# Row sums of squares moved into the last output tile, one modulation sum moved, and idle products reshaped, in a three-block transformer kernel

## The reference

```
for i in range(2):                       # first_block
    mod = silu(c) @ ada_w[i] + ada_b[i]  # sh1, sc1, g1, sh2, sc2, g2
    h = rmsnorm(x, norm1_g[i]) * (1 + sc1) + sh1
    y = attention_i(h)                   # i=0: window + sinks, i=1: stick breaking
    x = x + g1 * y
    h = rmsnorm(x, norm2_g[i]) * (1 + sc2) + sh2
    x = x + g2 * ((silu(h @ w_gate[i]) * (h @ w_up[i])) @ w_down[i])
u = rmsnorm(x, norm_mix_w)               # second_block
x = x + hybrid_mixer(u)
x = x + conv_gated_mlp(rmsnorm(x, norm_ffn_w))
return rmsnorm(x, final_norm_w)
```

## Time and profile before

| | |
|---|---|
| median of three runs | 2357.7 us |
| the profiled execution, its own time | 2357.86 us |
| its span, first to last instruction | 2356.0 us |
| PE busy / weight loads busy | 2289.3 us (97%) / 1830.7 us (78%) |
| DVE / ACT / POOL busy | 1170.3 / 870.5 / 163.1 us |
| mean granted clock of TensorE | 0.992 |

### The profile page before, as it was taken

The page is one execution under the profiler, slowest core; times in us unless marked ns, Lnnn a source line. Parts: engine busy times, 40 slices in busy tenths (PEclk is TensorE's granted clock), DMA queues, the critical chain, the costliest instruction groups (busy, mean ns, idle before and its releaser), DMA issues.

```text
span 2356.0 us, 27370 instructions
## 1 busy us (share of the span) xinstructions
PE 2289.3 (97%) x11168; PEld 1830.7 (78%) x11168; DVE 1170.3 (50%) x1621; ACT 870.5 (37%) x1413; POOL 163.1 (7%) x145
## 2 busy tenths in 40 slices
PE   7988999999999999999999999999999999999998
PEld 4767788888777677888887877866778887888886
DVE  5764655543465744333335455556744345553453
ACT  3653322222354533322323236356363223332331
POOL 2111000000100010000010002022020001000001
PEclk9999999999999999999999999999999999999999
DMA  9422465633212122232232222211223222233222
GB/s 339 141 90 84 167 223 196 212 110 99 81 63 72 48 70 88 91 99 99 91 106 81 98 91 95 98 59 63 72 90 108 98 81 99 90 98 107 93 87 81
DMA packets 77517, 250.67 MB, mean 106 GB/s; under 512 B 8272, under 2 KB 16720, under 8 KB 77392
## 3 DMA queue, kind: packets, MB, share of 16 engines
q1 hardware_dynamic: 77392, 248.93, 31.4%
HBM read 244.70 MB, written 4.19 MB: 106 GB/s over the span
## 4 chain that ended last, share of the span: by engine, by line
PE 88%; ACT 5%; DVE 4%; issue 1%; POOL 1%; DMA 0%; POOLq 0%; DVEq 0%; SPq 0%; ACTq 0%
PE pb L755 26%; PE pb L759 26%; PE pb L757 25%; PE pb L967 1%; PE pb L992 1%; PE pb L800 1%; PE pb L977 1%; PE pb L943 1%; ACT slab L1371 1%; ACT whi L1118 1%; PE pb L779 1%; PE pb L775 1%; PE pb L777 1%; ACT spare L1371 1%; PE pb L1042 1%
## 5 line engine op out<-in xcount | busy, mean ns | idle before, releaser
L755 PE MATMUL pb<-hhi,whi 128*128 128x512 f32 x1976 | 785.7, 398 | 5.0 <-ACT hhi L1146 3.0
L1410 DVE TENSOR_TENSOR wlo<-raw,whi 128x1024 fp32r<-128x1024 f32 x361 | 446.4, 1241 | 673.2 <-ACT whi L1118 673.1
L757 PE MATMUL pb<-hhi,wlo 128*128 128x512 f32 x1976 | 770.5, 390 | 1.7 <-DVE wlo L1410 1.7
L759 PE MATMUL pb<-hlo,whi 128*128 128x512 f32 x1976 | 771.0, 390 | 0.4 <-DVE hlo L1406 0.4
L1118 ACT ACTIVATE whi<-raw 128x1024 fp32r<-128x1024 f32 x361 | 379.2, 1056 | 728.7 <-PE pb L759 712.0
L755 PEld LDWEIGHTS pb<-hhi,whi 128*128 128x128 f32 x1976 | 370.8, 188 | 98.1 <-issue 24.3
L759 PEld LDWEIGHTS pb<-hlo,whi 128*128 128x128 f32 x1976 | 370.7, 188 | 81.4 <-DVE hlo L1406 1.6
L757 PEld LDWEIGHTS pb<-hhi,wlo 128*128 128x128 f32 x1976 | 371.1, 188 | 78.9 <-DVE wlo L1410 2.7
L755 PE MATMUL pb<-ahi,whi 128*128 128x512 f32 x848 | 336.6, 397 | 1.4 <-ACT ahi L1300 0.7
L759 PE MATMUL pb<-alo,whi 128*128 128x512 f32 x848 | 331.9, 391 | 0.0
L757 PE MATMUL pb<-ahi,wlo 128*128 128x512 f32 x848 | 331.5, 391 | 0.0
(11 more groups left out here) (231 smaller groups left out, 1686.0 us busy)
## 6 DMA issues: line engine op xcount, KB each, us to landing
raw<-stream SPq DMA_DIRECT2D x361, 512.0 KB, 3.3
slab<-ada_w SPq DMA_DIRECT2D x80, 512.0 KB, 4.9
early<-ada_w SPq DMA_DIRECT2D x32, 256.0 KB, 8.5
X<-xT SPq DMA_DIRECT2D x8, 256.0 KB, 4.8
ya<-slab SPq DMA_DIRECT2D x8, 256.0 KB, 2.7
slab<-ya SPq DMA_DIRECT2D x8, 256.0 KB, 4.7
outT<-X SPq DMA_DIRECT2D x8, 256.0 KB, 2.1
cst<-consts SPq DMA_DIRECT2D x1, 576.0 KB, 8.6
```

Of the source, the lines that this page charges most:

```text
L755: e.matmul(out, wh, hi, start=s.k == 0, stop=False)
L757: e.matmul(out, wl, hi, start=False, stop=False)
L759: i = e.matmul(out, wh, lo, start=False, stop=s.last)
L1410: e.tensor_tensor(wlo[:, u % NW, :], raw[:, u % NRAW, :], whi[:, u % NW, :].bitcast(F), ALU.subtract).then_inc(*v_cut.up(u))
```

## The change

`gemm` takes the number of the norm that follows as `hold`, and emits a new tick `sums` behind block k = K - 3 of its last output tile. `sums` holds the first half of the old `total`; `total` keeps the second half. For norm 0 and the group norms `sums` stands directly ahead of `total`, as before. `modsum(11)` moves to the end of the `mods()` generator, two generator steps behind the last `fma`; the generator is woven into the feed-forward product, one step to six blocks. `warm` issues two matmuls, with 512 and 256 columns, in place of one with 512.

```
@@ gemm
             self.tick("mm", Step(u, b, k, k == K - 1, tile, src(k), rows))
+            if hold and (k, m) == (K - 3, len(outs) - 1):
+                self.tick("sums", hold)
@@ mods
                 tick("fma", 8 * j + k)
                 yield 1
+        yield 1
+        tick("modsum", 11)
@@ rstd, norm (and the same for norm 6)
     def rstd(sid):
+        if sid == 0 or isinstance(sid, tuple):
+            tick("sums", sid)
         tick("total", sid)
...
-        tick("warm", 1)
+        tick("warm", 768)
         rstd(n)
-        tick("warm", 1)
+        tick("warm", 768)
         tick("spread", n)
-        tick("warm", 1)
+        tick("warm", 768)
@@ project, project_first, ffn
-        run(gemm(src, K, outs(4), "m", then=squares, hold=True))
+        run(gemm(src, K, outs(4), "m", then=squares, hold=n))
...
-                                    hold=part and d0 == 4)
+                                    hold=n + 1 if part and d0 == 4 else None)
@@ ahead of norm(2)
     run(mod)
-    tick("modsum", 11)
@@ tensor
-        def total(sid):
-            b = take(("stat", sid))
+        def sums(sid):
+            b, n = take(("stat", sid)), nstat(sid)
             w.wait_ge(d_in, "vec")
-            n = 3 if isinstance(sid, tuple) else 7
             w.wait_ge(v_norm if sid == 0 else p_sum, (sid, n - 1))
             for c in range(4):
-                i = e.matmul(b[:, c:c + 1], acc[:, quarter(c)], C("one"), start=c == 0, stop=False, skip_group_check=True)
+                e.matmul(b[:, c:c + 1], acc[:, quarter(c)], C("one"), start=c == 0, stop=False, skip_group_check=True)
+
+        def total(sid):
+            b, n = bank(("stat", sid)), nstat(sid)
             w.wait_ge(a_sq, (sid, n))
             for c in range(4):
                 i = e.matmul(b[:, c:c + 1], sq_of(sid, n)[:, quarter(c)], C("one"), start=False, stop=True, skip_group_check=True)
...
             b = take("warm")
-            for _ in range(n):
-                e.matmul(b, ident, cst[:, 0:S], start=True, stop=True)
+            for m in (S, n - S):
+                e.matmul(b[:, 0:m], ident, cst[:, 0:m], start=True, stop=True)
```

More of the change, by code:

```diff
@@ L121, in release, with gemm @@
         self.held.clear()
-    def gemm(self, src, K, outs, order="k", rows=P, evac=None, then=None, hold=False):
+    def gemm(self, src, K, outs, order="k", rows=P, evac=None, then=None, hold=None):
         M = range(len(outs))
@@ L328, in project_first @@
         order += [(k, m) for m in range(5, 8) for k in range(KD)]
-        steps = gemm(lambda k: ("oa", k), KD, [("wo_a", P * i, ("res", 0, i)) for i in range(8)], order, then=squares, hold=True)
+        steps = gemm(lambda k: ("oa", k), KD, [("wo_a", P * i, ("res", 0, i)) for i in range(8)], order, then=squares, hold=1)
         def as_ready():
@@ L1070, in output @@
             give(("y", g, j), v_ssd, ("y", g, j))
-        do = {"mm": mm, "mr": mr, "evac": evac, "modsum": modsum, "pre": pre, "premod": premod, "total": total, "warm": warm, "spread": spread, "norm": norm,
+        do = {"mm": mm, "mr": mr, "evac": evac, "modsum": modsum, "pre": pre, "premod": premod, "sums": sums, "total": total, "warm": warm, "spread": spread, "norm": norm,
               "tables": tables, "kstat": lambda: head_stats("k"),
```

## The result

The changed kernel took 2362.84 us in the median of 16 runs (2359.35 to 2364.97), the kernel before 2357.8 us beside it (2355.22 to 2359.03). The ratio is 1.0021, 95% interval 1.0014 to 1.0029: slower by 5.0 us, just past the 0.2% that I had set as the bound; I had given "slower" 0.19 and "the same" 0.77. The interval, 3.3 to 6.8 us, has that bound inside it. Forecast was 2360.5 us, +2.8, with a range of 2357.2 to 2363.4; both measurements lie in it, the first near its upper end.

What follows compares the result with a forecast made beforehand. PE, busy for 97% of the span, was taken as the bound. Stream passes +5.1, `modsum(11)` +1.71, norm 2 -1.73 and clock -2.3 made +2.8 us on 2357.7: 2360.5 us, range 2357.2 to 2363.4.

Steps and rivals of the forecast that it cites:

- The passes in the stream: Last tile ahead of each of six norms: eight one-column passes paid in full, 0.85 us each group, +5.1 us.
- `modsum(11)`: In the first feed-forward product's stream: the modulation sum costs +1.71 us and waits for nothing.
- the first part: The passes over `acc` move from the gaps into the last tile ahead of six norms: 6 x 0.85 = +5.1 us.
- rival B: In the products' streams: one-column passes slip in cheaply between wide matmuls, 0 to 0.2 us for eight; 2355.3 us; 8%.
- That the gaps win nothing: Gaps of norms 1 and 3 to 6: ACT's square sets the passes' start; moving `acc` passes frees 0 to 0.05 us, taken 0.
- Norm 2: Gap of norm 2: without modulation sum and `acc` passes, the passes over the square start 1.73 us earlier.
- The wait for POOL: `sums` in the last tile: POOL's sixth addition ends 0.2 us before it is needed; wait taken as 0.
- The cover of the idle products: Gaps of the norms: at full clock each 768-column idle product fits, cost 0; the second has only 0.2 us cover.
- The clock: Norms 1, 2 and 6: wider idle products hold full clock and give back 2.3 us, bounds 0 and 2.3.
- Rival A: At the norms: the clock still falls and longer idle products become the wait; 2362.8, about 2363.6 or 2365 us; 16%.
- C: Last tiles at three norms: `sums` waits for POOL, 0.3 to 1 us each; 2361.4 to 2363.5 us; 9%.
- D: Outside the norms: half-speed stretches vanish in the changed kernel's runs; faster by over 0.2%; 3%.

Runs made afterwards that it cites:

- f1: The changed kernel measured a second time, beside the kernel before on one chip: 2361.87 us, ratio 1.0015.
- f2: Changed kernel with the `acc` passes back in the gap and the first idle product at 512 columns, the others 768: 2356.33 us, ratio 0.9991 to the kernel before.
- e1: Changed kernel with idle products back at 512 columns and `modsum(11)` back ahead of norm 2, so only `sums` moved: 2362.54 us, ratio 1.0024 to the kernel before.
- g1: Changed kernel with `sums` behind block K - 5 in place of K - 3, six matmuls sooner: 2364.29 us, ratio 1.0027 to the kernel before.
- e2: Kernel before with 768 columns in all idle products, everything else as before: 2356.57 us, ratio 1.0001.
- e3: Kernel before with only `modsum(11)` moved into the first feed-forward product: 2356.89 us, ratio 1.0001.
- e4: Kernel before with second and third idle products at 768 columns, and `modsum(11)` replacing norm 2's third idle product: 2359.4 us, ratio 1.0010.
- f4: Kernel before without any idle product at norms 1 to 6: 2367.59 us, ratio 1.0038.

## Why the prediction was right in kind and short in size

**The passes in the stream**, the main term, was right in mechanism and sized 8% short: 0.92 us for each group, not 0.85 (5.5 us in all, not 5.1). I had read the step that holds the passes, and not the step behind it: a 512-column matmul that follows one-column passes gives 0.1 us less room than usual to the next. The sign of it stood in the trace of before: from 407.23 the next matmul was 0.31 us away. Per pass that is 0.115 us in the stream. The same holds for `modsum(11)`, +1.8 us, not 1.71. f1 against f2 gives the first part its price by time: 5.5 us, give or take one (f2's first idle product is also 256 columns narrower, which shows in no distance).

By the Trainium skill, "TensorE: Matmul & The Clock Gate", section "Back-to-back issue gap", the issue floor of a matmul of 1 to 64 columns is about 25 ns. The same section says that its gaps are those of an isolated matmul and, at small sizes, leave the weight load out; the prediction took the figure without that condition as the price of rival B. Here every pass loads 128 columns of weights, and the trace gives 0.11 us from one start to the next, over four times the floor, in agreement with the condition. That the number of columns that are moved hardly matters here can be read from the changed kernel: its eight one-column passes from 886.41 and its eight 128-column passes of the spread from 888.91 both follow one another at 0.11 us.

**That the gaps win nothing** was right: 1.94 us from last matmul to the passes over the square at norms 1, 3 and 4 before and after, and in e1; 1.88 to 1.89 us at norms 5 and 6. PE's wait for ACT grew from nothing that shows to 0.26 us.

**Norm 2** was right: 1.75 us sooner, against 1.73.

**The wait for POOL** was right at 0, and g1 gives the room that I had read, 0.2 us.

**The cover of the idle products** was right: nothing was late in any of the six gaps at full clock. My reading that 768 columns fit "even with nothing in between" was a condition: e2 shows that with the `acc` passes in between they don't. I had also written that the trace shows no pass of 256 columns; it has some, over 64 rows (lines 915 and 967), which I had overlooked. Nothing hung on it: the 256-column passes of the idle products took half of a 512-column one, as taken.

**The clock** was the uncertain term, -2.3 us. That it holds at the norms was right in both traces of the changed kernel, and in that of g1. What it gives back in the medians is the static +5.6 less the measured +5.0 and +3.6: 0.6 and 2.0 us, each uncertain by about 2 us. The weak step here is that I took what the one profiled execution of before had lost at its norms as the gain of a median; by the traces with 512 columns throughout it lost three norms (before) or one (e3), and each execution has half clock in other places too, worth up to 4 us in the table above. The 2.2 us between forecast and first measurement are 0.5 us of undersized passes and, as what is left, about 1.7 us of clock; against the second measurement (+3.6) it is 0.8 us in all. So the passes are shown to be undersized, while the size of the clock's share stays open within its noise, and that the second measurement came closer is luck as much as insight.

Rival A did not come: no norm fell in the two traces. That the first measurement, 2362.84 us, equals A's 2362.8 for a clock gain that is not earned is chance: A took a static price 0.5 us lower and a clock that falls. B falls with e1 and f1 against f2. C did not come: no trace of the changed kernel shows a wait ahead of `sums`. D's condition, half clock elsewhere, moves single executions both ways.

## What to carry to other kernels

Before moving work out of a gap, look at which engine ends the gap. If another one does, work of a full engine is free inside the gap and is paid in full in the stream; here the same eight passes cost 0 us under ACT's square and 0.92 us in the product. Filling the gap with wider idle work was worth about 2 us (f2, 0 to 4) when it did not push what stood behind it, and nothing that can be told from none when it did (e2). The price of a wait in a stream is the distance between the starts on either side of it, less the usual one, and not the idle time in a profile's bracket (1.14 and 0.92 us in g1). A step moved within one common list of ticks has to be checked on every engine that walks the list, as DVE in e4.

## What the runs showed of the hardware

- In f4 the gaps held 16 one-column passes and the eight of a spread, and no wide matmul. TensorE stood at half clock at norms 1 to 5 and stayed there for up to 10.3 us; each of these gaps took 8.2 to 9.0 us. The idle products of 0.86 us, 17 in all, are worth 9.3 us over the kernel (5.9 to 12.0).
- A float32 pass of 256 columns takes 0.22 us at full clock (888.27 to the next at 888.48 in the second idle product of norm 3), half of a 512-column one (0.43), and the four passes delayed nothing.
- Passes that load 128 columns of weights follow one another at 0.11 us at full clock, with 1 column or with 128 moved. Before 18 us, in both traces, the one-column passes stood 0.21 us apart. The first 512-column matmul behind a group of one-column passes is followed by the next after 0.31 to 0.32 us in place of 0.23, at full clock in every such place of these traces.
- At the very start the profile gives the clock as 1.00 in stretches whose rows are twice as long as in the other execution (the first spread, at 20 us: 2.07 us after and 1.16 us before): the duration of rows, not the clock column, tells the level there.
- Runs of one kernel span 2 to 6.5 us (0.1 to 0.3%); in the two traces compared by place, what the change did not do came from where half clock fell. The medians of the kernel before moved by 1.4 us between batches.
